# Seven half-size products in place of full block products in the merge-gate stage of a hybrid encoder layer

## The reference

```python
xn = _rms_norm(x, lp['g_mix'])
proj = xn @ lp['w_in']          # ... | gate_m | gate_r, 2048 columns each
y_ssm = _rms_norm(y_ssm.reshape(b, L, SSM_INNER) * jax.nn.silu(z.astype(f32)), lp['g_ssm']).astype(x.dtype)
o_m = y_ssm @ lp['w_out_m']
o_r = (h.astype(x.dtype) * jax.nn.gelu(gate_y)) @ lp['w_out_r']
mixed = jax.nn.sigmoid(gate_m) * o_m + jax.nn.sigmoid(gate_r) * o_r
x = x + mixed @ lp['w_o']
```

## Time and profile before

| | us |
|---|---|
| median of three runs | 3063.0 (3062.35 to 3067.26) |
| the profiled execution | 3060.54 |
| its span, first to last instruction | 3059.0 |
| merge stage, first matmul to first matmul of the tails | 976.44 to 1636.92 |
| first matmul of the `w_o` product | 1645.75 |

### The profile page before, as it was taken

The page is one execution under the profiler, slowest core; times in us unless marked ns, Lnnn a source line. Parts: engine busy times, 40 slices in busy tenths (PEclk is TensorE's granted clock), DMA queues, the critical chain, the costliest instruction groups (busy, mean ns, idle before and its releaser), DMA issues.

```text
span 3059.0 us, 33611 instructions
## 1 busy us (share of the span) xinstructions
PE 2862.9 (94%) x14019; PEld 1853.8 (61%) x14019; DVE 529.9 (17%) x1100; ACT 387.0 (13%) x723; POOL 50.9 (2%) x78
## 2 busy tenths in 40 slices
PE   7889999899999999999999998989889989888898
PEld 4556555555555555555557875655555556555787
DVE  3333333323322000000000002100010000000212
ACT  2212121212222000000001111000000000000312
POOL 0000000000000000000001000000000000000000
PEclk9999899999999999999999998999999999999999
DMA  4444343332332332233335426999999999999631
GB/s 137 137 136 141 109 124 106 120 94 91 91 114 82 110 100 92 90 102 110 110 110 183 153 98 271 419 412 428 429 425 412 421 429 427 429 430 415 227 102 42
DMA packets 228968, 646.87 MB, mean 211 GB/s; under 512 B 7804, under 2 KB 196756, under 8 KB 210004
## 3 DMA queue, kind: packets, MB, share of 16 engines
q1 hardware_dynamic: 209904, 598.89, 51.4%
q0 software_dynamic: 6528, 27.56, 2.8%
q10 hardware_dynamic: 12490, 19.79, 1.7%
HBM read 616.18 MB, written 30.04 MB: 211 GB/s over the span
## 4 chain that ended last, share of the span: by engine, by line
PE 83%; DMA 12%; DVE 2%; issue 1%; ACT 1%; SPq 0%; DVEq 0%; POOL 0%; ACTq 0%; POOLq 0%
PE bank L1401 22%; PE bank L1291 13%; PE bank L1371 11%; DMA arena<-in_w_exp_down_dram 9%; PE bank L1516 8%; PE bank L1501 7%; PE bank L1480 6%; PE bank L1440 6%; PE bank L1542 5%; PE bank L1351 1%; PE bank L1546 1%; DMA arena<-in_state_ssm_dram 1%; DMA arena<-in_w_in_dram 1%; DMA out_dram<-arena 0%; PE bank L1337 0%
## 5 line engine op out<-in xcount | busy, mean ns | idle before, releaser
L1401 PE MATMUL bank<-arena 128*128 128x384 f32 x2048 | 660.6, 486 | 0.0
L1401 PEld LDWEIGHTS bank<-arena 128*128 128x128 f32 x2048 | 389.1, 190 | 271.4
L1501 PE MATMUL bank<-arena 128*64 128x256 f32 x4096 | 449.7, 380 | 23.8 <-DVE arena L1111 16.7
L1291 PE MATMUL bank<-arena 128*128 128x384 f32 x1280 | 418.2, 489 | 10.8 <-DMA arena<-in_w_in_dram 9.5
L1501 PEld LDWEIGHTS bank<-arena 128*64 128x64 f32 x4096 | 301.2, 137 | 172.1 <-issue 28.6
L1291 PEld LDWEIGHTS bank<-arena 128*128 128x128 f32 x1280 | 244.2, 191 | 181.7 <-DMA arena<-in_w_in_dram 10.1
L1371 PE MATMUL bank<-arena 128*128 128x384 f32 x1024 | 330.9, 486 | 0.0
L1516 PE MATMUL bank<-arena 128*64 128x512 f32 x1024 | 253.2, 652 | 57.5 <-DMA arena<-in_w_exp_down_dram 44.4
L1371 PEld LDWEIGHTS bank<-arena 128*128 128x128 f32 x1024 | 194.8, 190 | 135.6 <-issue 0.5
L1516 PEld LDWEIGHTS bank<-arena 128*64 128x64 f32 x1024 | 79.2, 149 | 210.9 <-issue 210.9
L1480 PEld LDWEIGHTS bank<-arena 128*128 128x128 f32 x1632 | 185.8, 194 | 17.0 <-issue 13.0
(11 more groups left out here) (328 smaller groups left out, 1319.5 us busy)
## 6 DMA issues: line engine op xcount, KB each, us to landing
arena<-in_w_exp_gate_dram SPq DMA_DIRECT2D x32, 4096.0 KB, 16.0
arena<-in_w_exp_up_dram SPq DMA_DIRECT2D x32, 4096.0 KB, 17.8
arena<-in_w_exp_down_dram SPq DMA_DIRECT2D x32, 4096.0 KB, 19.3
arena<-in_w_in_dram SPq DMA_DIRECT2D x48, 2048.0 KB, 8.3
arena<-in_w_out_m_dram SPq DMA_DIRECT2D x8, 2048.0 KB, 8.2
arena<-in_w_out_r_dram SPq DMA_DIRECT2D x8, 2048.0 KB, 8.2
arena<-in_w_o_dram SPq DMA_DIRECT2D x8, 2048.0 KB, 8.4
expert_rows<-arena ACTq DMA_DIRECT2D x64, 256.0 KB, 13.5
```

The lines of the kernel that those rows point to most:

```text
L1291: last = mm(banks[(m + c) % 2][:, 0:T], w[:, k, c * 128:(c + 1) * 128], xnT[:, k, :], start=(k == 0), stop=(k == KC - 1))
L1401: last = mm(banks[2 * s + cc][:, 0:T], slab[s % 2][:, k, cc * 128:(cc + 1) * 128], rhs[:, k, :], start=(k == 0), stop=(k == KC - 1))
L1501: last = mm(banks[2 * x + i][h * SLOTS:(h + 1) * SLOTS, 0:FF // 2], xe[:, k, x * SLOTS:(x + 1) * SLOTS], w[:, k, h * (FF // 2):(h + 1) * ( ...
```

## The change

The output of a slab, 256 x 384, is seen as 2 x 2 blocks of 128 x 192, the slab as 2 x 2 blocks of 1024 (k) x 128 and the activations as 2 x 2 blocks of 1024 x 192. In place of eight block products, seven are made, of sums of blocks (Strassen's scheme in Winograd's form). Each product is 8 matmul calls of 192 moving columns. This is done for 31 of the 32 slabs; the first, gate_m of turn 0, is still made of 32 calls of 384 columns.

- VectorE makes four sums of weight blocks per slab (`slab_sums`), 128 x 1024 floats each: three into `sums` (two sets, one per parity), the fourth in place. The sums of slab w+1 stand ahead of the work on the products of slab w in its program.
- Pool makes four sums of each activation matrix (`second_operands`), 128 x 1536 floats each, one in place: for `Y` and one for `xnT` after the SSD groups' last store, three more for `xnT` after slab 0, four for `H` after slab 15. TensorE waits for them (`t_ready`) at slabs 1, 2 and 17.
- ScalarE copies products 0 and 1 out of PSUM, VectorE adds the other five to what it has, quadrant by quadrant (`quadrants`), into the gate tiles `sg` or, times the gate, into `mixed`. ScalarE's sigmoid then works in place in SBUF.
- Every product takes the next of the eight banks in turn, and waits until the product that used the bank eight products before has been read.
- The waits for `rs_ms` and for the first sigmoid stand ahead of slab 1 now. A slab's load waits for the seven products of the slab two before. The first `w_o` slab's load waits for slab 30, the second's for slab 31, and the tails wait for ScalarE's last copy.
- The loops are written out: 31 times on each engine, with no branch.

```diff
+            for w in range(SLABS):
+                gate, gate_at, out, _ = MIX[w // 16]
+                i = (w % 16) // 2
+                if w < 2:
+                    sp.wait_ge(proj_done, 72 + 2 * w)
+                else:
+                    sp.wait_ge(mix_mm, 2 + NP * (w - 2))
+                sp.dma_start(slab[w % 2], cols(a[out], i * SLAB) if w % 2 else cols(a[gate], gate_at + i * SLAB)).then_inc(slab_loaded[w % 2], 16)
...
             for b in range(8):
+                if b < 2:
+                    sp.wait_ge(mix_mm, 2 + NP * (SLABS - 2 + b))
                 load_slab(b % 2, a["w_o"], b * SLAB, wo_mm, max(3 * b, 1))
...
+            def second_operands(m, q2, q3, q4, at, part):
+                (b11, b12), (b21, b22) = halves(m)
+                if part != 1:
+                    sub(q3, b22, b12, ALU.subtract).then_inc(t_ready, 1)
+                if part != 0:
+                    pool.wait_ge(t_ready, at + 1)
+                    sub(b12, b12, b11, ALU.subtract).then_inc(t_ready, 1)
+                    pool.wait_ge(t_ready, at + 2)
+                    sub(q2, b22, b12, ALU.subtract).then_inc(t_ready, 1)
+                    pool.wait_ge(t_ready, at + 3)
+                    sub(q4, b21, q2, ALU.subtract).then_inc(t_ready, 1)
+
+            pool.wait_ge(y_act, KC)
+            pool.wait_ge(hn_stored, 16 * KC)
+            second_operands(Y, y2, y3, y4, 0, None)
+            second_operands(xnT, x2, x3, x4, 4, 0)
+            pool.wait_ge(mix_mm, 2)
+            pool.wait_ge(l_done, GROUPS + 1)
+            second_operands(xnT, x2, x3, x4, 4, 1)
+            pool.wait_ge(mix_mm, 2 + NP * 15)
+            second_operands(H, y2, y3, y4, 8, None)
...
+            def slab_sums(w):
...
+                dve.wait_ge(slab_loaded[w % 2], 256 + 16 * (w // 2) + 16)
...
+                TT(s1, a21, a22, ALU.add).then_inc(w_sums, 1)
+                dve.wait_ge(w_sums, at + 1)
+                TT(s2, s1, a11, ALU.subtract).then_inc(w_sums, 1)
+                dve.wait_ge(w_sums, at + 2)
+                TT(s4, a12, s2, ALU.subtract).then_inc(w_sums, 1)
+                TT(a21, a11, a21, ALU.subtract).then_inc(w_sums, 1)
...
+                def put(c, half, value):
+                    dst = mixed[:, k + c, half]
+                    if w < 16:
+                        return TT(dst, value, sg[c][:, half], ALU.mult)
+                    xlink(TT(value, value, sg[c][:, half], ALU.mult))
+                    return TT(dst, dst, value, ALU.add)
+
+                dve.wait_ge(part_out, 2 * (w - 1) + 2)
+                read(2, u2, p1)
+                xlink(TT(u4, u2, p5, ALU.add))
+                read(3, sg[0][:, hi] if gate else u4, u4)
+                read(4, u3, u2)
+                xlink(TT(sg[1][:, hi] if gate else p5, u3, p5, ALU.add))
...
+            def product(w, n, stationary, moving):
...
+                for k in range(HK):
+                    last = mm(bank, stationary[:, k, :], moving[:, k, :], start=(k == 0), stop=(k == HK - 1))
+                last.then_inc(mix_mm, 1)
+
+            pe.wait_ge(l_sig, KC + 2)
+            pe.wait_ge(y_act, KC)
+            pe.wait_ge(rs_ms, 1)
+            for w in range(1, SLABS):
...
+                pe.wait_ge(slab_loaded[w % 2], 256 + 16 * (w // 2) + 16)
+                pe.wait_ge(t_ready, 4 if w == 1 else 8 if w < 17 else 12)
+                if w == 1:
+                    pe.wait_ge(mix_sig, 1)
+                at = 4 * (w - 1)
+                product(w, 0, a11, b11)
+                pe.wait_ge(w_sums, at + 1)
+                product(w, 1, s1, b12)
+                pe.wait_ge(w_sums, at + 2)
+                product(w, 2, s2, q2)
+                pe.wait_ge(w_sums, at + 3)
+                product(w, 3, s4, b22)
+                pe.wait_ge(w_sums, at + 4)
+                product(w, 4, a21, q3)
+                product(w, 5, a12, b21)
+                product(w, 6, a22, q4)
+
+            pe.wait_ge(part_out, 2 * (SLABS - 1))
```

More of the change, by code:

```diff
@@ L103, in hybrid_stream_step @@
         tokcol = v3(keep.take(10 * HEADS), 10)
+        lru_h0_at = keep.at
         lru_h0 = v3(keep.take(128), NSEQ)
@@ L143, in hybrid_stream_step, with quad, halves, product_bank @@
         lw = v3(slot[2][:, 0:1024], 8)
-        rm = Region(3 * SLABF, SLABF)
-        sg_m, sg_r, t_m, t_r = ([rm.take(T) for _ in range(2)] for _ in range(4))
+        HK, HT, NP = KC // 2, T // 2, 7
+        MIX = [("w_in", OFF_GM, "w_out_m", 0), ("w_in", OFF_GR, "w_out_r", 0)]
+        SLABS = 32
+        QUAD = HK * HT
+        def quad(at):
+            return v3(arena[:, at:at + QUAD], HK)
+        def halves(m):
+            return [[m[:, k * HK:(k + 1) * HK, t * HT:(t + 1) * HT] for t in range(2)] for k in range(2)]
+        y2, y3, y4 = quad(9216), quad(9216 + QUAD), quad(21504)
+        x3, x2, x4 = quad(23040), quad(12288), quad(12288 + QUAD)
+        sums = [[v3(arena[:, 15360 + (3 * b + i) * 1024:15360 + (3 * b + i + 1) * 1024], HK) for i in range(3)] for b in range(2)]
+        sg = [arena[:, 8192 + c * T:8192 + (c + 1) * T] for c in range(2)]
+        spare = tokcol.rearrange("p a b -> p (a b)")
+        p1, u2 = spare[:, 0:HT], arena[:, lru_h0_at - HT + 128:lru_h0_at + 128]
+        u3, p5 = ss_acc[:, 0:HT], ss_acc[:, HT:T]
+        u4 = arena[:, 8192 + 2 * T:8192 + 2 * T + HT]
+        def product_bank(w, n):
+            return banks[(NP * (w - 1) + n + 2) % 8][:, 0:HT]
         rd = Region(3 * SLABF, SLABF)
@@ L508, in _ @@
                 store_h(jj, jj % 2)
-            pool.wait_ge(mix_mm, 4 * KC + 2)
+            sub = nc.gpsimd.tensor_tensor
+            def second_operands(m, q2, q3, q4, at, part):
[18 more added lines that the diff above has]
+            second_operands(H, y2, y3, y4, 8, None)
+            pool.wait_ge(mix_mm, 2 + NP * (SLABS - 1))
             pool.wait_ge(tails_T, 11)
@@ L697, in _ @@
             act.wait_ge(l_done, GROUPS + 1)
[L698 to L704, removed]
+            for cc in range(2):
+                act.wait_ge(mix_mm, cc + 1)
+                last = A(sg[cc], banks[cc][:, 0:T], ACT.Sigmoid)
+            last.then_inc(mix_sig, 1)
+            for w in range(1, SLABS):
+                act.wait_ge(quads_done, w - 1)
+                for n, dst in enumerate((p1, p5)):
+                    act.wait_ge(mix_mm, 2 + NP * (w - 1) + n + 1)
+                    A(dst, product_bank(w, n), ACT.Copy).then_inc(part_out, 1)
+                if w % 2 == 0:
+                    act.wait_ge(quads_done, w)
+                    A(sg[0], sg[0], ACT.Sigmoid)
+                    A(sg[1], sg[1], ACT.Sigmoid).then_inc(mix_sig, 1)
             for q in range(10):
@@ L1036, in _ @@
             link(V.reciprocal(rstdB, rstdB))
[L1039 to L1051, removed]
+            xlink = Chain(dve, mixch)
@@ new lines, in slab_sums @@
+            def slab_sums(w):
+                s1, s2, s4 = sums[w % 2]
+                (a11, a21), (a12, a22) = [[slab[w % 2][:, k * HK:(k + 1) * HK, n * 128:(n + 1) * 128] for n in range(2)] for k in range(2)]
+                dve.wait_ge(slab_loaded[w % 2], 256 + 16 * (w // 2) + 16)
+                if w > 2:
+                    dve.wait_ge(mix_mm, 2 + NP * (w - 2))
+                at = 4 * (w - 1)
[5 more added lines that the diff above has]
+                TT(a21, a11, a21, ALU.subtract).then_inc(w_sums, 1)
@@ new lines, in quadrants, with read @@
+            def quadrants(w):
+                k = 2 * ((w % 16) // 2)
+                lo, hi = slice(0, HT), slice(HT, T)
+                gate = w % 2 == 0
+                if not gate:
+                    dve.wait_ge(mix_sig, (w + 1) // 2)
+                    if w < 16:
+                        TT(sg[0], sg[0], rstdB, ALU.mult)
+                        xlink(TT(sg[1], sg[1], rstdB, ALU.mult))
+                def read(n, dst, other):
+                    dve.wait_ge(mix_mm, 2 + NP * (w - 1) + n + 1)
+                    TT(dst, other, product_bank(w, n), ALU.add).then_inc(part_read, 1)
+                    dve.wait_ge(part_read, 5 * (w - 1) + n - 1)
+                def put(c, half, value):
+                    dst = mixed[:, k + c, half]
+                    if w < 16:
+                        return TT(dst, value, sg[c][:, half], ALU.mult)
[7 more added lines that the diff above has]
+                xlink(TT(sg[1][:, hi] if gate else p5, u3, p5, ALU.add))
+                if not gate:
+                    put(0, hi, u4)
+                    put(1, hi, p5)
+                read(5, sg[0][:, lo] if gate else p1, p1)
+                if not gate:
+                    put(0, lo, p1)
+                read(6, sg[1][:, lo] if gate else u3, u3)
+                if not gate:
+                    put(1, lo, u3).then_inc(mix_done, 1)
+                    dve.wait_ge(mix_done, 2 + (w + 1) // 2)
+                dve.sem_inc(quads_done, 1)
@@ L1053, in _ @@
+            slab_sums(1)
+            for w in range(1, SLABS):
+                if w + 1 < SLABS:
+                    slab_sums(w + 1)
```

(19 more changed lines are left out.)

18 lines of the change are left out of this document (10 added, 8 removed).

## The result

The changed kernel takes 2990.4 us (median of four runs, 2988.21 to 2997.7) against 3064.17 us for the kernel before (four runs, 3062.35 to 3067.26): a ratio of 0.9768, 95% interval 0.9756 to 0.978. The forecast was 2990. Its profiled execution took 2992.45 us (span 2990.9), 68.1 less than the one before.

The account below looks back on a forecast made before the run. TensorE's matmul records were taken to bound the merge stage; 20.64 + 0.9 + 563.9 + 3.0 + 7.45 = 595.9 us against 669.3, a gain of 73.4. From 3060.5 that gave 2987.1, plus 2.5 for the median, 2990; range 2982 to 3008.

Parts of the forecast that it names:

- The rate: Merge stage matmuls: a line through 256 and 384 columns gives 162.4 ns a record at 192; 3472 records take 563.9 us.
- the 4.8 ns more: Excess of the 128-column row over the line's 109.1 ns; left out at 192 columns, kept as upper end, 167.2 ns.
- the small hold-up: Rival: the merge stage's shorter matmuls are held up a little, 167.2 ns a record, +16.6 us, 3006; chance 0.17.
- the unhidden load at 190 ns: Rival: weight load not hidden under a short matmul, a pair costs 190 ns, +95.8 us, 3085; chance 0.04.
- VectorE hidden: Merge slabs: VectorE's sums and product work take at most 14.0 of 18.2 us, priced at nothing under TensorE.
- The start: Start of merge stage: waits for `rs_ms` and sigmoid have one slab as cover; TensorE resumes near 998.0, +0.9 us.
- the slow Pool: Rival: Pool's activation sums take 7.2 us each, not 3.6, +13.3 us at `xnT` and `H`, 3003; chance 0.08.
- VectorE beside Pool: Merge stage, both engines at once: Pool's `xnT` instructions may hold up sums, 0 to 5.9 us; middle taken, +3.0.
- that they shut each other out in turn: Rival: each Pool `xnT` instruction holds up a VectorE sum in turn, 5.9 us in place of 3.0, 2993; chance 0.25.
- The five early Pool instructions: Start of the LRU groups: 18 us of Pool work hidden by four groups' projections on TensorE; otherwise up to 18 us.
- The end: After the stage: 8.41 us `w_o` wait goes, tails next late; `w_o` product starts after 7.45, not 8.83; worth 1.4 us.
- The sum: Stage's first matmul to that of `w_o`: 669.3 before, 595.9 after; gain 73.4 us, median 2989.6, rounded to 2990.

Follow-up runs that it names:

- the kernel with the late load: Against the changed kernel, the first `w_o` slab is asked for only when the stage's last product has ended; 2992.84 us against 2990.83.

## Why the prediction was right, step by step

*The rate* was the step that carried the sum. 162.4 ns from the line, 162.6 measured; 563.9 us forecast for 3472 records, 564.4 where they run without a wait. The reason given for taking the line and not the 4.8 ns more (another pace holds at 128 columns than at 192) is borne out by the two runs with fewer columns. Two readings behind it were weaker than they looked. That loads are back to back is no sign that they set the pace: at 192 columns they are too (551.00 of 551.00 us), and there the line holds. And of the 4.8 ns only 2.3 are the pace (111.4 against 109.1); the rest is in the row itself, whose piece of 96 records also holds the end of its last one (an estimate: 95 distances of 111.4 ns and one record of some 0.3 us make the 10.93 us). Two rivals fall with the 162.6 ns, the small hold-up and the unhidden load at 190 ns: the single load still lasts 190 ns, and one starts every 162.6.

*VectorE hidden* held: at most 14.0 us a slab was the estimate, 26.24 in two slabs with doubled sums was no limit, and without doubling it is busy 261 of 551 us.

*The start.* The sigmoid's wait was forecast at 0.9; TensorE went on at 1002.21, 0.83 after slab 0's 20.64 us. Pool's instruction was put at 3.6 us; it takes 3.43 where nothing disturbs it, so the slow Pool falls too, and the estimate of 3.4 from the Trainium skill's GPSIMD Engine Reference, section Elementwise, agrees.

*VectorE beside Pool* is the step that was mis-sized: 3.0 taken as the middle of 0 and 5.9, 4.9 measured. The rival, that they shut each other out in turn, was the true mechanism. Its price came out below 5.9 for two reasons that the rows show: Pool's instruction is 3.43 and not 3.6, and a turn of one sum and one Pool instruction lasts 4.3 to 4.4 us (sums start at 1001.88, 1006.16 and 1010.54, so 4.28 and 4.38 apart), less than the 4.65 of 1.22 and 3.43 laid end to end. The rule of the Trainium skill (SBUF - State Buffer, Who interferes with whom) agrees in kind: two SBUF inputs against a reading Pool instruction clash, one operand in a bank or a Pool that only writes does not. For `H` the forecast of no wait held (Pool 14.9 us in all, TensorE in one piece), and the doubled sums (2.06 us of waiting) and the shorter slabs of the runs with fewer columns (3.2 and 3.3) show that this cover is not large.

*The five early Pool instructions* do slow VectorE, as the timeline of the changed kernel's first LRU group shows:

```profile
632.75 3.42 POOL L540 TENSOR_TENSOR arena<-arena 128x1536 f32<-128x1536 f32 x1 [4.62 <-DMA out_dram<-arena]
...
632.90 3.31 DVE L966 COPY arena<-arena 128x3 f32 x1 [5.78 <-DMA out_dram<-arena]
```

A copy of three floats per partition lasts 3.31 us; the kernel before, with Pool at rest, has this shape at 0.16 in its first LRU group. But the next LRU group starts 89.21 us after the first in both kernels (619.11 to 708.32, 623.40 to 712.61): the cover that was named held, and the cost is nothing.

*The end.* The preload was put at 1.4 us and not 8.4, since the tails were next late; 1.3 measured by undoing it. The stage's end to the `w_o` product: 7.45 forecast, 7.24 measured.

*The sum.* Stage with tails 595.9 forecast, 598.1 measured: 1.9 for the clash, the rest in tenths. The 1.7 us of the first `w_o` block, which were named and not counted, came in, though not for the reason given. These two nearly cancel, which is luck, and so is the agreement of the medians' 73.8 us with the 73.4 forecast: the later rounds of the same two kernels gave 68.4 (3059.26 to 2990.83) with the same 598.1 us in the stage. What repeats from trace to trace is 71.2 us in the stage and 1.7 in the first `w_o` block; the times around it move by some 4 us, in the SSD stage and behind the start of the `w_o` product.

## What to carry to other kernels

A scheme that trades products for sums is worth its record count times the rate of the *new* shape; read that rate from stretches of several shapes, and ask of each shape whether its pace still follows the columns, since below that point fewer columns bring nothing (111.4 ns at 128 columns and at 96). When a wait goes, name what is next late before pricing it: of an 8.4 us load only 1.3 were to be had. Elementwise work that is handed to Pool is free only away from VectorE's SBUF instructions that the critical path wants; one more wait in Pool's program won 4.9 us here.

## What the runs showed of the hardware that was not expected

- Pool's reading instructions hold up not only VectorE's two-input instructions in SBUF (1.22 to 4.3 us) but a plain SBUF copy of three floats (0.16 to 3.31 us), while VectorE instructions with an operand in a bank run beside them at 0.37.
- The granted clock stayed at 1.00 through a gap of 8.7 us with 5.8 busy in the kernel with the late load, and fell to 0.64 behind a like gap in the kernel before. With the sums doubled it fell to 0.50 behind a wait of 12.4 us; behind the changed kernel's waits of 1.1 to 1.5 us it stayed at 1.00.
- The same SSD code ends up to 5.4 us apart from trace to trace (618.37 to 623.79), and the granted clock in it tells which: 0.95 in 400 to 500 us in the early ones, 0.90 in the late ones.
- Records of 128 and of 96 columns follow each other at the same 111.4 ns at full clock, while a single weight load shows 190 ns and loads are back to back at 192 columns as well.
